# One core, two hybrid transformer blocks: in the turned gate and up steps, pairs of a 512- and a 256-column product in place of two sweeps

## The reference, cut to what matters

```python
h = rms_norm(x, norm_ffn[l])
x = x + (jax.nn.silu(h @ w_gate[l]) * (h @ w_up[l])) @ w_down[l]
```

## Time and profile before

| | |
|---|---|
| median of 3 runs | 1422.94 us (1422.38 to 1423.04) |
| profiled execution, its own time | 1422.92 us |
| its span, first to last instruction | 1421.1 us |
| PE busy | 1411.0 us (99%) |
| DVE, ACT busy | 992.5 us (70%), 835.5 us (59%) |
| granted clock of TensorE, mean | 0.998 |
| HBM over the span | 172 GB/s |
| L931 in the chain that ended last | 21% of the span |
| L935 in it | 11% |
| L570, L573, L576 in it | 19%, 18%, 18% |

### The profile page before, as it was taken

One profiled execution on the slowest core, in us unless ns is written; L12 is line 12 of the kernel. 1 busy time (PEld: TensorE's weight loads), 2 busy tenths in 40 slices (PEclk: granted clock), 3 DMA queues, 4 the chain that ended last, 5 costly groups with the idle time before them and its releaser, 6 DMA issues.

```text
span 1421.1 us, 20878 instructions
## 1 busy us (share of the span) xinstructions
PE 1411.0 (99%) x8226; PEld 1200.3 (84%) x8226; DVE 992.5 (70%) x1366; ACT 835.5 (59%) x1337; POOL 80.7 (6%) x86
## 2 busy tenths in 40 slices
PE   9999999999999999999999999999999999999998
PEld 8887888888888878888888888888888888888886
DVE  5698766676567987666666788666666788666665
ACT  7775555544567654555555788454545788555553
POOL 0113200000002220000000000000000000000001
PEclk9999999999999999999999999999999999999999
DMA  8754456666375445476664524567653634556661
GB/s 286 223 154 122 159 163 195 200 197 192 111 227 178 149 135 164 153 214 203 187 194 140 172 89 163 178 193 223 190 182 108 221 104 139 178 188 194 195 191 57
DMA packets 174512, 245.51 MB, mean 173 GB/s; under 512 B 18880, under 2 KB 117840, under 8 KB 174416
## 3 DMA queue, kind: packets, MB, share of 16 engines
q1 hardware_dynamic: 174224, 244.11, 54.7%
q10 hardware_dynamic: 192, 0.08, 0.0%
HBM read 243.10 MB, written 1.05 MB: 172 GB/s over the span
## 4 chain that ended last, share of the span: by engine, by line
PE 96%; DVE 2%; ACT 1%; issue 0%; POOL 0%; POOLq 0%; ACTq 0%
PE misc L931 21%; PE acc L570 19%; PE acc L576 18%; PE acc L573 18%; PE misc L935 11%; PE misc L664 3%; DVE w_lo L1470 1%; PE misc L672 1%; PE misc L706 1%; PE misc L731 1%; DVE arena L1920 1%; PE misc L884 1%; PE misc L883 1%; PE misc L881 0%; PE misc L685 0%; PE misc L785 0%
## 5 line engine op out<-in xcount | busy, mean ns | idle before, releaser
L1470 DVE TENSOR_TENSOR w_lo<-w_raw,w_hi 128x1024 fp32r<-128x1024 f32 (+2 forms) x466 | 551.3, 1205 | 219.4 <-ACT w_hi L1050 217.5
L1050 ACT ACTIVATE w_hi<-w_raw 128x1024 fp32r<-128x1024 f32 (+2 forms) x466 | 473.1, 1038 | 244.0 <-PE misc L935 171.5
L931 PE MATMUL misc<-h_both,w_hi 128*128 128x512 f32 x1280 | 319.7, 392 | 0.0
L931 PEld LDWEIGHTS misc<-h_both,w_hi 128*128 128x128 f32 x1280 | 232.7, 189 | 43.3
L570 PE MATMUL acc<-w_hi,h_both 128*128 128x512 f32 (+2 forms) x768 | 206.5, 390 | 0.5 <-ACT h_both L1089 0.5
L576 PE MATMUL acc<-w_hi,h_both 128*128 128x512 f32 (+2 forms) x768 | 198.8, 380 | 1.0 <-DVE h_both L1511 1.0
L573 PE MATMUL acc<-w_lo,h_both 128*128 128x512 f32 (+2 forms) x768 | 198.8, 380 | 0.0
L935 PEld LDWEIGHTS misc<-h_both,w_lo 128*128 128x128 f32 x1280 | 174.6, 190 | 12.5
L935 PE MATMUL misc<-h_both,w_lo 128*128 128x256 f32 x1280 | 178.5, 282 | 0.0
L576 PEld LDWEIGHTS acc<-w_hi,h_both 128*128 128x128 f32 x768 | 140.7, 188 | 28.8 <-DVE h_both L1511 2.1
L573 PEld LDWEIGHTS acc<-w_lo,h_both 128*128 128x128 f32 x768 | 140.8, 188 | 27.6 <-DVE w_lo L1470 0.2
(11 more groups left out here) (237 smaller groups left out, 1180.0 us busy)
## 6 DMA issues: line engine op xcount, KB each, us to landing
w_raw<-in_w_in SPq DMA_DIRECT2D x112, 512.0 KB, 4.5
w_raw<-in_w_gate SPq DMA_DIRECT2D x176, 256.0 KB, 3.1
w_raw<-in_w_up SPq DMA_DIRECT2D x176, 256.0 KB, 3.8
w_raw<-in_w_down SPq DMA_DIRECT2D x88, 512.0 KB, 4.0
w_raw<-in_w_out SPq DMA_DIRECT2D x40, 512.0 KB, 3.5
w_raw<-in_w_in SPq DMA_DIRECT2D x16, 336.0 KB, 4.6
w_raw<-in_w_proj_a SPq DMA_DIRECT2D x8, 512.0 KB, 3.9
w_raw<-in_w_proj_b SPq DMA_DIRECT2D x8, 512.0 KB, 4.2
```

Source lines behind the costliest of these rows:

```text
L931: pe.matmul(bank[:, :], w_hi[:, r, cols], h_both[:, tile, :, :].rearrange("p u t -> p (u t)"), start=tile == 0, stop=False)
L1050: act.activation(w_hi[:, g % RING, 0:w], w_raw[:, g % RING, 0:w], ACT.Copy)\
L1470: dve.tensor_tensor(w_lo[:, g % RING, 0:w], w_raw[:, g % RING, 0:w], w_hi[:, g % RING, 0:w].bitcast(F32), ALU.subtract)\
```

## The change

In `gate_up_turned` the wait for `w_lo` moves in front of the first product of a step, and the loop over the cells runs once. It issues the long product of a cell and right behind it the short one, where there were two loops over the cells. The operands, the banks, the number of products and the mark on the last of them stay. Nothing changes on the other engines. As a line goes away, L931 becomes L932, L935 becomes L934, and the lines behind it move up by one.

```diff
                         r = (g + q) % RING
                         pe.wait_ge(*AC.of("hi", g + q))
+                        pe.wait_ge(*DV_.of("lo", g + q))
                         for bank, tile, cols in cells:
                             pe.matmul(bank[:, :], w_hi[:, r, cols], h_both[:, tile, :, :].rearrange("p u t -> p (u t)"),
                                       start=tile == 0, stop=False)
-                        pe.wait_ge(*DV_.of("lo", g + q))
-                        for bank, tile, cols in cells:
                             mm = pe.matmul(bank[:, T:2 * T], w_lo[:, r, cols], h_hi[:, tile, :], start=False,
                                            stop=tile == KD - 1)
                         mm.then_inc(*PE.slot("used", g + q))
```

## The result

The changed kernel takes 1429.45 us (median of 4 runs, 1429.41 to 1429.62), the kernel before 1422.99 us in the same comparison: **slower by 6.5 us**, ratio 1.0046 with a 95% interval from 1.0034 to 1.0059. The forecast was 1420.5, range 1411 to 1429. The span of the profiled execution went from 1421.1 to 1427.6 us, at a granted clock of 0.998 and 0.999, so the clock has no part in it.

What follows compares the result with a forecast made beforehand. The prediction took PE as the bound, its time nearly the number of products times their spacing. Terms of -1.9 us (order) and -0.5 us (sweep behind a group), others 0, sum to -2.4 from 1422.9: 1420.5 us, range 1411 to 1429.

Steps and rivals of the forecast that it cites:

- the first part: Spacing of PE's products: 226.8 ns at 512 columns, 173.3 at 384; the line through them gives 120.0 at 256.
- Part 1: Order of products in the turned steps: with pairs at the line, 160 steps cost 443.7 us against 445.6, -1.9 us.
- Part 2: Sweep behind a group of turned steps: half of its extra 1.0 us goes, -0.5 us.
- Parts 3 to 6: Turned steps: earlier w_lo wait, extra wait instruction, same bank twice running, and the banks' readers; nothing gained or lost.
- Rival A: Short sweep is held by its loads and pairs hide them: pair 341.2 ns, -8.8 us, 1414.1 us; chance 0.25.
- Rival C: Lateness behind a change of length becomes permanent on every long product: pair 352.5 ns, +5.6 us, 1428.5 us; chance 0.28.

## Why the prediction was wrong

**The step that failed is in the first part: it took the 120.0 ns of the line through 384 and 512 columns as the 256-column product's own time, left the loads out, and let a pair run at 346.7 ns.** Since the short sweep shows 119, I called the short product no dearer than its columns. With half loads it takes 113 to 114 ns, so 6 to 7 ns of the 120 come with the full load beside it. And the pairs, with full loads, take 353.5 ns.

The line itself is no accident of two points. The kernel before also has products of 336 columns, which it puts at 153.3 ns:

```profile
390.71 0.77 PE L576 MATMUL acc<-w_hi,h_both 128*128 128x336 f32 x4
...
402.30 1.09 PE L570 MATMUL acc<-w_hi,h_both 128*128 128x512 f32 x4
```

Between these starts lie 76 of them, at 152.5 ns. But every product on the line has a full load beside it and neighbours of its own length. Its points can't show what a load adds, nor what happens when the lengths alternate. With half loads a pair is 340 ns, 227 for the long product and 113 for the short one, some 0.44 ns a column for either. Two lengths don't make a law, and the 384-column products were not run with half loads.

**Part 1** (-1.9 us from pairs at 346.7 ns): they came out at 353.5. The call grew by 0.14 us where the forecast had it shrink by 0.05.

**Part 2** (-0.5 us from the sweep behind a call): it went the other way, 5.503 us against 5.467 by the unrounded starts, about +1.3 us over the 40 calls.

**Parts 3 to 6** held. Neither the earlier wait nor the second one costs anything (1422.86 us with both in the old order), the bank doesn't matter (352 ns a pair with another bank, 346.9 for equal lengths in the same one), and no wait appeared on PE at the turned lines.

**Rival A** was half right: the short sweep is slower by its loads (120 ns against 114 with half ones). But I let the pair hide them, and it didn't. Beside the short product runs the load of the next *long* one, with 128 columns like every other. The order of the products changes whose load it is and not how long it is.

**Rival C**, with 0.28, is what happened: the long product behind a short one is late every time. Its price was 352.5 ns a pair against 353.5 measured, and 1428.5 us against 1429.45, the difference being mostly the down sweeps that it left out. Some luck is in so close a hit: the parts were 232.5 and 120 ns, where 236 and 117 were measured. Its reason was only half true. It isn't a change of length as such that costs: runs of two have half as many changes as the pairs, and twice as many as runs of four, and are cheaper than both. The evidence that I set against it, the 10 ns that the short sweep seems to give back, was mostly the first short product of a sweep, which takes 113 ns where the later ones take 119 or 120.

The Trainium skill, *TensorE: Matmul & The Clock Gate*, section "Step-by-step: what each phase is for", says that loading the next stationary operand takes no SBUF read bandwidth from the running product. I had read this as a load that costs nothing, which is more than it says: here a full load beside a 256-column product costs 7 to 13 ns a pair. Whether the running product is slowed or the next one has to wait for its load, no record shows.

The section "LDWEIGHTS (loading the stationary operand)" of the same page of the Trainium skill gives columns / 1.2 ns for a load, as an estimate 107 ns for 128 columns and 53 for 64. The load records agree with the difference: their medians are 188 or 189 ns for 128 columns and 134 to 138 for 64. By that estimate alone a full load would still fit beside a product of 113 ns, with 6 ns to spare, so it makes the tight place plausible and doesn't account for the cost.

**What stays open.** Why a full load beside the *long* product, which has 227 ns, costs 7 ns a pair when the one beside the short product is full too, and nothing otherwise (the first two lines of the table against the last two). Why a long sweep behind a short one is late even when the short one has half loads. Why the first pair of a call, at 0.34 us, and the first short product of a sweep, at 113 ns, pay nothing with full loads. And why runs of two settle into a cheaper pattern than runs of four or one. The spacings repeat exactly from call to call, so it is a matter of how loads and products stand to each other in time, but that is argued, and no record here shows the inside of a load.

## What to carry to other kernels

When PE streams without a pause, look at the load that runs beside each product, not at the product's own. In this kernel an alternation of long and short products left a full load beside every short one, and made the long ones late. A line through longer products with the same loads can't show the load's share in a short one; a run with half the stationary columns can. If short products must be, try them in one long run, with long ones at the end of the stage: here that was worth 0.16% where pairs lost 0.46%.

## What the runs showed that was not expected

- A product of 256 columns with a stationary side of 128 takes 120 ns in a run and 114 with one of 64 (0.95 and 0.91 us for eight).
- Halving the stationary side of the short product in the pairs brings the pair from 353.5 to 346.7 ns, though that load has the long product's time to hide in. Halving that of the long one brings it to 340.
- Pairs, runs of two, of four and of eight of the same products give 1429.45, 1421.74, 1425.55 and 1422.86 us: the cost of an order isn't monotone in its changes.
